# A ring of expert weights: two neighbouring pieces asked for in one 1 MB transfer instead of two of 512 KB

## The chip, the cores and the metric

The kernel runs on one core of a Trainium2 chip, as one launch. The metric is the device time of that launch in microseconds (us). Three runs of the kernel before took 1549.37, 1553.48 and 1554.05 us; their median is 1553.48 us.

## The reference, cut to what matters

The program is one layer of an encoder: modulated norm, an input projection, a retention branch and a differential attention branch, an output projection, and then a mixture of 16 experts over 640 tokens (512 of a prompt, 8 x 16 of samples). The change touches only the expert part:

```python
# hf: 640 tokens x 1024; w1, w3: 16 x 1024 x 512; w2: 16 x 512 x 1024; every token goes to 2 of the 16 experts
for e in range(N_EXPERTS):
    ff = (jax.nn.silu(hf @ w1[e]) * (hf @ w3[e])) @ w2[e]
    y = y + combine[:, e:e + 1].astype(hf.dtype) * ff
```

All of it is float32. The weights of one expert are 3 x 2 MB, so 16 experts read 100 MB of HBM, each byte once.

## The kernel before, in words

**Tiling.** An expert gets a block of up to 128 token rows, fetched by an indirect DMA from GpSimd (POOL) into `xe` and turned on TensorE (PE) into `xT`. The weights come in pieces of 128 partitions x 2 x 512 float32, 512 KB, 12 per expert: four of W3, four of the next expert's W1, four of W2. Pieces are numbered in the order of use; 0 to 3 (W1 of expert 0) have buffers of their own, 4 to 191 go through a ring of 12 slots (`RING`, line 1261; `slot`, line 1350). For an expert e from 0 to 14 W3 is pieces 12e+4 to 12e+7, W1 of e+1 is 12e+8 to 12e+11, and W2 is 12e+12 to 12e+15 (the last experts differ a little, line 1267).

**The life of a piece n.** Products of float32 are made of three matmuls on float32r parts (`mm3`, line 91), so each piece is split first:

1. SyncE (SP) waits until TensorE has used piece n-12, which had the same slot, and issues the DMA into `raw` (lines 1401 to 1403).
2. ScalarE (ACT) waits for the landing and writes the high part, `hi` (line 1454).
3. VectorE (DVE) writes the low part, `lo`, over the raw data (line 1536).
4. TensorE runs six matmuls of 512 columns (lines 93 to 95 by way of `up`, line 1639, or `down`, line 1647) and counts `used`.

Each slot has a semaphore `loaded` of its own (line 1353).

**Order on each engine.** All is written out by hand. ACT and DVE walk through steps m = 0, 1, ... and split piece m+4 in step m (`LEAD`), with their other work at fixed places between (lines 1479 to 1505 and 1575 to 1590). What matters here is the product of the two hidden activations, `multiply` (line 1553, the row L1556 of a profile): it stands on DVE right behind the low part of piece 12e+11. TensorE needs it after two of the four W1 pieces of the next expert, when it turns the product (`turn_a`, line 1631; rows L1636):

```python
for p in range(4):
    if p == 2:
        turn_a(e)                                     # waits for multiply(e)
    up(first_piece("W1", e + 1) + p, p, self.U, e + 1)
```

SP's queue also sends each expert's finished 512 KB of rows to HBM (`send_y`, line 1413), before the pieces 28, 40, 52, ... It waits before piece 8 for the token rows of expert 0 (line 1400). One more user of the DMA engines is the indirect fetch of `xe` (line 1427).

Of the kernel before, what the change touches and what calls it, by code (L numbers as in the profile page):

```python
# [24 lines left out]
F32 = mybir.dt.float32  # L25
# [7 lines left out]
P = 128  # L33
# [19 lines left out]
W = 512  # L53
# [7 lines left out]
class Map:  # L61


    def __init__(self, nc, start, end):
        self.nc, self.at, self.end = nc, start, end
# [1195 lines left out]
RING, LEAD, EARLY, PIECES = 12, 4, 12, 12 * N_EXP  # L1261
# [3 lines left out]
def first_piece(kind, e):  # L1265

    return {"W1": 12 * e - 4 if e else 0, "W3": 12 * e + (4 if e < N_EXP - 1 else 0), "W2": 12 * e + (12 if e < N_EXP - 2 else 16 if e < N_EXP - 1 else 8)}[kind]


class Experts:  # L1270


    def __init__(self, nc, io, K, ctx, banks):
        self.io, self.K = io, K
        sem = lambda name: K.semaphore("m_" + name)
        many = lambda name, n: [sem(f"{name}{i}") for i in range(n)]
        base, hT, wt = K.phase_base, K.hT_at, K.wts_at
        piece = lambda name, at, dt=F32: nc.alloc_sbuf_tensor_at("m_" + name, [P, 2, W], dt, offset=at)
        row = lambda name, at: nc.alloc_sbuf_tensor_at("m_" + name, [P, D_MODEL], F32, offset=at)
        at = [base + 49152 + 4096 * p for p in range(3)] + [base + 88064]  # L1280
        self.raw0 = [piece(f"raw_first{p}", at[p]) for p in range(4)]
        self.lo0 = [piece(f"lo_first{p}", at[p], F32R) for p in range(4)]
        self.hi0 = [piece(f"hi_first{p}", base + 4096 * p, F32R) for p in range(4)]
        at = [hT + 4096 * i for i in range(8)] + [wt + 4096 * i for i in range(4)]
        self.raw = [piece(f"raw{i}", at[i]) for i in range(RING)]
        self.lo = [piece(f"lo{i}", at[i], F32R) for i in range(RING)]
        self.gx = [[row(f"gx{a}_{t}", at[a * NT + t]) for t in range(NT)] for a in range(2)]
        hi_at = [wt + 16384 + 4096 * i for i in range(4)] + [base + 16384] + [base + 71680 + 4096 * i for i in range(4)] \
            + [base + 20480 + 4096 * i for i in range(3)]
        self.hi = [piece(f"hi{i}", hi_at[i], F32R) for i in range(RING)]  # L1290
        sb = Map(nc, hT + 32768, hT + 40960)
        self.xe = [sb(f"m_xe{i}", [P, D_MODEL], F32) for i in range(2)]
        sb = Map(nc, wt + 32768, wt + 49152)
        self.xT = [[sb(f"m_xT{i}_{n}", [P, KT, P], F32R) for n in ("hi", "lo")] for i in range(2)]
        sb = Map(nc, wt + 32768, wt + 36864)
        last_aT = tuple(sb(f"m_aT_last_{n}", [P, 4, P], F32R) for n in ("hi", "lo"))
        sb = Map(nc, base + 32768, base + 40960)
        self.su = sb("m_su", [P, W], F32)
        self.aT_hi = sb("m_aT_hi", [P, 4, P], F32R)
        self.aT_lo = sb("m_aT_lo", [P, 4, P], F32R)  # L1300
        self.aT = [(self.aT_hi, self.aT_lo)] * (N_EXP - 1)
        self.aT.append(last_aT)
        sb = Map(nc, base + 40960, base + 49152)
        self.yst = [sb(f"m_yst{i}", [P, D_MODEL], F32) for i in range(2)]
        sb = Map(nc, base + 61440, base + 71680)
        self.gt2 = sb("m_gt2", [P, 2, D_MODEL], F32)
        self.cf = sb("m_cf", [P, 5, 2, NT], F32)
        self.wv = sb("m_wv", [P, 2, NT], F32)
        self.ci = sb("m_ci", [P, 2, NT], I32)
        self.si = sb("m_si", [P, N_EXP], I32)  # L1310
        self.prod = sb("m_prod", [P, 2, NT, N_EXP], F32)
        sb = Map(nc, K.after_small, K.sbuf_end)
        self.iota = sb("m_iota", [P, P], F32)
        self.posm = sb("m_posm", [P, NT, N_EXP], F32)
        self.tok_in = sb("m_tok_in", [P, NT, 2], F32)
        self.tok = nc.alloc_sbuf_tensor_at("m_tok", [P, NT, 2], BF16, offset=sb.at)
        assert sb.at + 32 <= K.sbuf_end
        self.oh = [nc.alloc_sbuf_tensor_at(f"m_oh{e}", [P, NT, P], BF16, offset=hi_at[6 + e // 3] + 1280 * (e % 3)) for e in range(N_EXP)]
        self.U, self.V, self.Y, self.T, self.AT, self.X = banks[0], banks[1], banks[2:4], banks[4:6], banks[6], banks[7]
        self.loaded0, self.hi0_done, self.lo0_done = many("first_loaded", 4), sem("first_hi_done"), sem("first_lo_done")  # L1320
        self.loaded, self.hi_done, self.lo_done = many("loaded", RING), sem("hi_done"), sem("lo_done")
        self.used, self.rounds_done, self.posm_done = sem("pieces_used"), sem("rounds_done"), sem("places_done")
        self.oh_done, self.slots_done, self.slots_taken = map(sem, ("chosen", "slots_done", "slots_taken"))
        self.xe_zero, self.go, self.xe_in, self.consts, self.tok_done = sem("xe_zero"), sem("pool_goes_on"), many("xe_in", 2), sem("consts_in"), sem("tok_done")
        self.link = sem("dve_link")
        self.t_done, self.t_hi, self.t_lo, self.su_done, self.a_done, self.at_done, self.at_hi, self.at_lo = map(
            sem, ("x_turned", "x_hi", "x_lo", "su_done", "a_done", "a_turned", "a_hi", "a_lo"))
        self.y_taken, self.y_out, self.ci_done, self.gath = sem("y_taken"), many("y_out", 2), sem("rows_found"), many("gathered", NT)
        self.weighed, self.summed, self.gated, self.added_up = map(sem, ("weighed", "summed", "gated", "added_up"))
        self.gt2_in, self.out, self.stored, self.h2_out = sem("gt2_in"), sem("rows_out"), sem("round_stored"), sem("h2_out")  # L1330
# [5 lines left out]
    def source(self, n):  # L1336
        if n < 4:
            w, e, p = "w1", 0, n
        else:
            e, i = (n - 4) // 12, (n - 4) % 12  # L1340
            p = i % 4
            w = ("w3", "w1", "w2")[i // 4]
            if n >= first_piece("W3", N_EXP - 1):
                e, w = ((N_EXP - 1, "w3"), (N_EXP - 2, "w2"), (N_EXP - 1, "w2"))[(n - first_piece("W3", N_EXP - 1)) // 4]
            e += w == "w1"
        if w == "w2":
            return self.io[w][0, e, p % 2 * 256:p % 2 * 256 + 256, p // 2 * W:(p // 2 + 1) * W].rearrange("(k r) n -> r k n", k=2)
        return self.io[w][0, e, p * 256:(p + 1) * 256].rearrange("(r k) n -> r k n", k=2)

    def slot(self, n):  # L1350
        return (n - 4) % RING

    def piece_loaded(self, r, n):
        s, k = self.slot(n), (n - 4) // RING
        return self.loaded[s], r * (16 * len(range(s + 4, PIECES, RING))) + 16 * k + 16

    def piece_used(self, r, n):
# [33 lines left out]
    def run_sp(self, sp):  # L1391
        io = self.io
        R = self.rounds(sp)
        with sp.Fori(0, R) as r:
            for n in range(4, PIECES):
                e = (n - 28) // 12
                if n >= 28 and (n - 28) % 12 == 0:
                    self.send_y(sp, r, e)
                if n == 8:
                    sp.wait_ge(*self.rows_in(r, 0))  # L1400
                if n - RING >= 4:
                    sp.wait_ge(*self.piece_used(r, n - RING))
                sp.dma_start(self.raw[self.slot(n)][:], self.source(n)).then_inc(self.loaded[self.slot(n)], 16)
            for e in range(N_EXP - 2, N_EXP):
                self.send_y(sp, r, e)
            for t in range(NT):
                sp.wait_ge(*self.added(r, t))
                out = io["o_y_p"][0, t * P:(t + 1) * P] if t < NP_T else io["o_y_s"].rearrange("b l d -> (b l) d")
                sp.dma_start(out, self.K.x1[:, t]).then_inc(self.out, 16)
            sp.wait_ge(self.out, r * (NT * 16) + NT * 16)  # L1410
            sp.sem_inc(self.stored, 1)
# [1492 lines left out]
```

## Time and profile before

| what | value |
|---|---|
| median of 3 runs | 1553.48 us |
| the profiled execution, its own time | 1547.23 us |
| its span, first to last instruction | 1545.4 us |
| mean granted TensorE clock | 0.990 of full speed |
| TensorE busy | 96% of the span |
| VectorE, ScalarE, GpSimd busy | 53%, 42%, 18% |
| HBM traffic | 197 GB/s over the span |
| ring transfers `m_raw<-w` in the trace | 188 of 512 KB, issued between 1208.8 and 1494.8 us |

The expert part runs from about 1208 us to the end. Shares over the whole span say little about it, since VectorE and the DMA engines are far busier there than before; it has to be read in windows of one expert. Matmuls are pipelined, so a busy time on TensorE overlaps from one to the next; the distance between two starts is the pace.

### The profile page before, as it was taken

How to read it: one execution, taken by the hardware profiler on the slowest of the kernel's cores; microseconds unless marked ns; L12 is line 12 of the kernel's file. 1: busy time of each engine (PE TensorE's matmuls, PEld its weight loads, DVE VectorE, ACT ScalarE, POOL GpSimd, SP SyncE). 2: the span in 40 equal slices, each digit the busy share in tenths (PEclk: the TensorE clock that was granted, in tenths of full speed). 3: DMA queues.
4: the chain of work that ended last, by engine and by line, in shares of the span. 5: the costliest groups of instructions: out<-in, count | busy, mean ns of one | idle time of the engine just before them, and what ended most of it. 6: DMA issues, size and time to landing. Idle time of an engine off the chain costs nothing.

```text
span 1545.4 us, 21620 instructions
## 1 busy us (share of the span) xinstructions
PE 1480.2 (96%) x7914; PEld 1124.5 (73%) x7914; DVE 812.2 (53%) x1424; ACT 649.5 (42%) x1073; POOL 284.7 (18%) x174
## 2 busy tenths in 40 slices
PE   8999999999999999999999899999999999999991
PEld 6775777577757775778777676677778878888880
DVE  4332441243125312221776867755365799999995
ACT  5313311331133113312445454544232478888881
POOL 2342224222322332233000000000222100000002
PEclk9999999999999999999999999999999999999996
DMA  9554465446544654432441254154841799999986
GB/s 350 185 141 160 161 196 138 158 161 206 138 149 161 206 145 141 151 108 70 169 136 55 69 188 141 42 157 151 287 122 42 267 329 407 404 398 396 398 327 231
DMA packets 149789, 302.92 MB, mean 196 GB/s; under 512 B 15867, under 2 KB 43691, under 8 KB 149557
## 3 DMA queue, kind: packets, MB, share of 16 engines
q1 hardware_dynamic: 145942, 291.06, 55.5%
q0 software_dynamic: 3744, 10.49, 1.9%
q8 instruction: 65, 1.06, 0.3%
q14 instruction: 38, 0.31, 0.1%
HBM read 257.84 MB, written 46.81 MB: 197 GB/s over the span
## 4 chain that ended last, share of the span: by engine, by line
PE 39%; DVE 5%; DMA 4%; issue 2%; ACT 1%; POOL 0%; DVEq 0%; ACTq 0%; POOLq 0%; SPq 0%
PE pj L93 10%; PE pj L95 10%; PE pj L94 10%; DMA m_raw<-w 2%; PE d_B L2564 1%; PE d_B L2583 1%; PE d_B L2591 1%; DVE d_tmp L2282 1%; DMA ring_raw<-w_in 1%; PE d_B L2625 1%; PE d_B L2573 1%; DMA d_kc<-cache_diff_k 1%; PE d_B L2731 1%; PE d_B L1636 1%; PE d_B L2602 1%
## 5 line engine op out<-in xcount | busy, mean ns | idle before, releaser
L93 PE MATMUL pj<-ring_hi,hT_hi 128*128 128x512 f32 x880 | 367.7, 418 | 5.3 <-ACT d_q_rows L2040 2.4
L95 PE MATMUL pj<-ring_hi,hT_lo 128*128 128x512 f32 x880 | 344.9, 392 | 0.0
L94 PE MATMUL pj<-ring_lo,hT_hi 128*128 128x512 f32 x880 | 344.0, 391 | 0.0
L511 POOL TENSOR_TENSOR ring_lo<-ring_raw,ring_hi 128x1024 fp32r<-128x1024 f32 x79 | 190.9, 2420 | 497.9 <-ACT ring_hi L585 497.8
L585 ACT ACTIVATE ring_hi<-ring_raw 128x1024 fp32r<-128x1024 f32 x79 | 83.3, 1057 | 365.3 <-DMA ring_raw<-w_in 353.2
L1536 DVE TENSOR_TENSOR m_lo<-m_raw,m_hi 128x1024 fp32r<-128x1024 f32 x188 | 222.1, 1221 | 20.9 <-ACT m_hi L1454 19.5
L93 PEld LDWEIGHTS pj<-ring_hi,hT_hi 128*128 128x128 f32 x880 | 165.7, 188 | 48.6 <-issue 15.0
L1454 ACT ACTIVATE m_hi<-m_raw 128x1024 fp32r<-128x1024 f32 x188 | 192.6, 1058 | 19.1 <-DMA m_raw<-w 16.1
L95 PEld LDWEIGHTS pj<-ring_hi,hT_lo 128*128 128x128 f32 x880 | 165.3, 188 | 36.5
L94 PEld LDWEIGHTS pj<-ring_lo,hT_hi 128*128 128x128 f32 x880 | 166.0, 189 | 28.3 <-issue 1.0
L782 DVE SCALAR_TENSOR_TENSOR r_S<-r_S,g,r_sm 128x512 f32<-128x512 f32 x64 | 45.0, 744 | 137.0 <-PE r_sm L1031 137.0
L93 PE MATMUL pj<-m_hi,m_xT_hi 128*128 128x512 f32 x248 | 98.0, 395 | 0.0
L95 PE MATMUL pj<-m_hi,m_xT_lo 128*128 128x512 f32 x248 | 96.9, 391 | 0.0
L94 PE MATMUL pj<-m_lo,m_xT_hi 128*128 128x512 f32 x248 | 96.5, 389 | 0.0
L2032 ACT ACTIVATE ring_hi<-ring_raw 128x1024 fp32r<-128x1024 f32 x37 | 39.2, 1058 | 66.7 <-DMA ring_raw<-w_in 25.3
L93 PE MATMUL pj<-ring_hi,r_oT_hi 128*128 128x512 f32 x160 | 64.3, 402 | 0.0
L94 PE MATMUL pj<-ring_lo,r_oT_hi 128*128 128x512 f32 x160 | 62.6, 391 | 0.0
L95 PE MATMUL pj<-ring_hi,r_oT_lo 128*128 128x512 f32 x160 | 62.3, 389 | 0.0
L1427 POOL DMA_INDIRECT m_xe<-xg,m_si x16 | 16.7, 1044 | 234.9 <-PE d_B L1628 215.5
L95 PEld LDWEIGHTS pj<-m_hi,m_xT_lo 128*128 128x128 f32 x248 | 46.5, 188 | 9.9
L94 PEld LDWEIGHTS pj<-m_lo,m_xT_hi 128*128 128x128 f32 x248 | 46.6, 188 | 9.3
L93 PEld LDWEIGHTS pj<-m_hi,m_xT_hi 128*128 128x128 f32 x248 | 46.6, 188 | 9.0
(363 smaller groups left out, 2353.3 us busy)
## 6 DMA issues: line engine op xcount, KB each, us to landing
m_raw<-w SPq DMA_DIRECT2D x188, 512.0 KB, 10.1
ring_raw<-w_in SPq DMA_DIRECT2D x72, 512.0 KB, 3.8
r_S<-state_ret SPq DMA_DIRECT2D x64, 256.0 KB, 4.6
r_ada_raw<-w_ada SPq DMA_DIRECT2D x16, 1024.0 KB, 6.8
o_state_s<-r_S SPq DMA_DIRECT2D x64, 256.0 KB, 4.4
a_raw<-w_ada SPq DMA_DIRECT2D x8, 1024.0 KB, 12.3
ring_raw<-w_in SPq DMA_DIRECT2D x32, 256.0 KB, 3.3
ring_raw<-w_br_ret SPq DMA_DIRECT2D x16, 512.0 KB, 4.2
```

What stands on the lines that cost most here:

```text
L93: pe.matmul(out, s_hi, m_hi, start=start, stop=False)
L94: pe.matmul(out, s_hi, m_lo, start=False, stop=False)
L95: return pe.matmul(out, s_lo, m_hi, start=False, stop=stop)
L511: pool.tensor_tensor(lo[:, p], raw[:, p], hi[:, p].bitcast(F32), ALU.subtract).then_inc(lo_done, 1)
L585: act.activation(hi[:, p], raw[:, p], ACT.Copy).then_inc(hi_done, 1)
L782: dve.scalar_tensor_tensor(S[:, u % 8], S[:, u % 8], K.g16[:, h:h + 1], job_bank("U", h, u)[:], ALU.mult, ALU.add) \
L1427: pool.indirect_dma_start(out=self.xe[e % 2][:], out_offset=None, in_=self.io["xg"][0:NT * P, :], in_offset=bass.IndirectOffsetOnAxis(ap=s ...
L1454: act.activation(self.hi[self.slot(n)][:], self.raw[self.slot(n)][:], ACT.Copy).then_inc(self.hi_done, 1)
L1536: dve.tensor_tensor(self.lo[s][:], self.raw[s][:], self.hi[s][:].bitcast(F32), ALU.subtract).then_inc(self.lo_done, 1)
L1636: last = pe.transpose(self.AT[:, a * P:(a + 1) * P], self.su[:, a * P:(a + 1) * P], K.ident[:])
L2032: act.activation(hi[:, p], raw[:, p], ACT.Copy).then_inc(hi_done, 1)
L2282: links(dve.tensor_tensor(tmp[:, m].rearrange("p (g c) -> p g c", c=DDH), x, bc(tabs[:, a, t, m].unsqueeze(1), [P, 8, DDH]), ALU.mult))
```

## The change

The twelve raw buffers of the ring become six pairs at the same addresses; the pairs are pieces (4, 5), (6, 7), ... SP's loop goes in steps of two. For a pair it waits until TensorE has used the second piece's predecessor, n-11, and issues one DMA of 128 partitions x 4 runs of 512 float32, 1 MB, which counts on the semaphore of the even slot. Both pieces of a pair wait for that one semaphore. The pieces on ACT, DVE and TensorE, and their order there, stay as they are.

In W1 and W3 a partition's share of a piece is two neighbouring rows, one run of 4 KB in HBM; of a pair it is two such runs, 512 KB apart. In W2 a partition's share of a piece is two half rows of 2 KB, and of a pair four of them, each 512 KB from the next.

```diff
-        self.raw = [piece(f"raw{i}", at[i]) for i in range(RING)]
         self.lo = [piece(f"lo{i}", at[i], F32R) for i in range(RING)]
+        self.raw_pair = [nc.alloc_sbuf_tensor_at(f"m_raw_pair{i}", [P, 2, 2, W], F32, offset=at[2 * i]) for i in range(RING // 2)]
+        self.raw = [self.raw_pair[i // 2][:, i % 2] for i in range(RING)]
...
-        if w == "w2":
-            return self.io[w][0, e, p % 2 * 256:p % 2 * 256 + 256, p // 2 * W:(p // 2 + 1) * W].rearrange("(k r) n -> r k n", k=2)
+        if n >= 4:
+            if w == "w2":
+                return self.io[w][0, e, :, p // 2 * W:(p // 2 + 1) * W].rearrange("(q k r) n -> r q k n", q=2, k=2)
+            return self.io[w][0, e, p * 256:(p + 2) * 256].rearrange("(q r k) n -> r q k n", q=2, k=2)
         return self.io[w][0, e, p * 256:(p + 1) * 256].rearrange("(r k) n -> r k n", k=2)
...
     def piece_loaded(self, r, n):
-        s, k = self.slot(n), (n - 4) // RING
+        s, k = self.slot(n) // 2 * 2, (n - 4) // RING
         return self.loaded[s], r * (16 * len(range(s + 4, PIECES, RING))) + 16 * k + 16
...
-            for n in range(4, PIECES):
+            for n in range(4, PIECES, 2):
                 e = (n - 28) // 12
                 if n >= 28 and (n - 28) % 12 == 0:
                     self.send_y(sp, r, e)
                 if n == 8:
                     sp.wait_ge(*self.rows_in(r, 0))
                 if n - RING >= 4:
-                    sp.wait_ge(*self.piece_used(r, n - RING))
-                sp.dma_start(self.raw[self.slot(n)][:], self.source(n)).then_inc(self.loaded[self.slot(n)], 16)
+                    sp.wait_ge(*self.piece_used(r, n + 1 - RING))
+                sp.dma_start(self.raw_pair[self.slot(n) // 2][:], self.source(n)).then_inc(self.loaded[self.slot(n)], 16)
```

## Rows read from the trace of the kernel before

**Rows 1.** The page: busy time per engine, and the span in 40 slices.

```profile
PE 1480.2 (96%) x7914; PEld 1124.5 (73%) x7914; DVE 812.2 (53%) x1424; ACT 649.5 (42%) x1073; POOL 284.7 (18%) x174
DMA  9554465446544654432441254154841799999986
```

**Rows 2.** Windows of one expert each: window, length, busy time (instructions), TensorE clock, DMA share, GB/s.

```profile
1230.00:1248.40 18.40, 18.40 (x88) 15.37 (x87) 16.63 (x18) 15.26 (x20) 0.99 (x1) 1.00 0.97 345
1248.40:1269.10 20.70, 17.94 (x85) 14.72 (x84) 19.60 (x34) 14.66 (x19) 0.99 (x1) 1.00 0.93 330
...
1286.92:1304.72 17.80, 17.80 (x86) 14.87 (x85) 16.59 (x17) 15.08 (x19) 0.99 (x1) 1.00 1.04 405
...
1358.12:1376.25 18.13, 18.01 (x86) 14.78 (x85) 16.48 (x17) 15.57 (x19) 0.99 (x1) 1.00 1.03 398
...
1412.03:1430.47 18.44, 18.01 (x86) 14.79 (x85) 16.33 (x17) 15.43 (x19) 0.99 (x1) 1.00 1.02 396
```

**Rows 3.** TensorE's timeline, two matmuls that follow each other: start, duration.

```profile
1356.16 0.39 PE L94 MATMUL pj<-m_lo,m_aT_hi 128*128 128x512 f32 x1
1356.39 0.39 PE L95 MATMUL pj<-m_hi,m_aT_lo 128*128 128x512 f32 x1
```

**Rows 4.** Waits from 1286.92 to 1448.44 us: who waited for whom, total, times, longest.

```profile
ACT m_hi L1454 <- DMA m_raw<-w: 12.6, 29, 1.1
DVE m_lo L1536 <- ACT m_hi L1454: 12.4, 30, 0.9
PEld d_B L1636 <- DVE m_su L1556: 2.3, 5, 0.9
```

**Rows 5.** The chain of waits from 1350 to 1367 us, around piece 95.

```profile
1351.06 11.69 DMA m_raw<-w
1362.74 0.02 issue
1362.76 1.07 ACT m_hi L1454
...
1365.00 0.69 DVE m_su L1556
...
1365.74 0.66 PE d_B L1636 x4
```

**Rows 6.** The same wait three experts on: the chain from 1404 to 1422 us.

```profile
1404.97 12.00 DMA m_raw<-w
```

**Rows 7.** Issues and landings of all DMAs from 1290 to 1440 us.

```profile
m_raw<-w SPq DMA_DIRECT2D x101, 512.0 KB, 10.4
yg<-m_yst SPq DMA_DIRECT2D x8, 512.0 KB, 10.8
```

**Rows 8.** SP's own waits over the span: who waited for whom, total, times, longest.

```profile
SPq L1403 <- PE pj L95: 177.9, 168, 8.0
```

**Rows 9.** ACT's timeline: two high parts without a wait.

```profile
1266.27 2.00 ACT L1454 ACTIVATE m_hi<-m_raw 128x1024 fp32r<-128x1024 f32 x2
```

**Rows 10.** DVE's timeline: the low parts of pieces 94, 95 and 96, 97.

```profile
1362.70 2.38 DVE L1536 TENSOR_TENSOR m_lo<-m_raw,m_hi 128x1024 fp32r<-128x1024 f32 x2 [0.57 <-ACT m_hi L1454]
...
1365.60 2.36 DVE L1536 TENSOR_TENSOR m_lo<-m_raw,m_hi 128x1024 fp32r<-128x1024 f32 x2
```

**Rows 11.** DVE's and TensorE's timelines: the product and its turn, experts 3 and 12.

```profile
1292.42 0.68 DVE L1556 TENSOR_TENSOR m_su<-m_su,pj 128x512 f32<-128x512 f32 x1
...
1294.26 0.60 PE L1636 MATMUL d_B<-ident,m_su 128*128 128x128 f32 x4
...
1454.98 0.68 DVE L1556 TENSOR_TENSOR m_su<-m_su,pj 128x512 f32<-128x512 f32 x1
...
1455.78 0.60 PE L1636 MATMUL d_B<-ident,m_su 128*128 128x128 f32 x4
```

**Rows 12.** SP's timeline: the issues of pieces 34 to 39.

```profile
1260.68 8.18 SPq L1403 DMA_DIRECT2D m_raw<-w  x6
```

**Rows 13.** DMA from 1262 to 1275 us, 40 slices of 0.325 us.

```profile
GB/s 366 416 429 403 315 277 252 315 340 328 164 82 44 107 233 246 265 221 233 164 170 277 340 397 397 378 366 303 265 63 82 139 158 258 366 353 353 384 422 410
```

## The prediction

> **What bounds the kernel now.** The page comes first, to find the stage. TensorE is busy for 96% of the span, VectorE for 53%, and the last slices of the DMA row, where the experts are, stand at 9, which nothing before them does for long [rows 1]. So the expert part is unlike the rest, and only its own windows count.
>
> The windows come next. From 1287 us an expert takes 17.80 us, and TensorE is busy through all of it, at a granted clock of 1.00; but the DMA share is 1.04 at 405 GB/s and VectorE works 16.59 us [rows 2]. Three resources are within 7% of one another. TensorE's pace is read from two starts, 0.23 us apart (0.227 over many), so a piece of six matmuls takes 1.36 us [rows 3]; twelve make 16.3, and turning rows and products takes the rest of 17.80. Some windows are longer, 18.13 and 18.44 us, with TensorE busy for 18.01 in both and the data at 396 to 398 GB/s [rows 2].
>
> The waits say who is late. Between 1287 and 1448 us ACT waited 29 times for a landing, 12.6 us in all; DVE waited 30 times for ACT, 12.4 us; TensorE's side lost 2.3 us, in five waits for the product L1556 [rows 4]. The chain shows how: piece 95 is issued at 1351.06, lands 11.69 us later, ACT splits it, DVE splits it, and only then comes the product (1365.00) that TensorE turns at 1365.74 [rows 5]. Piece 131 does the same with 12.00 us [rows 6].
>
> Is a landing slow by latency or by a queue? A ring transfer takes 10.4 us in the median from 1290 to 1440 us [rows 7], and one is issued about every 1.48 us (17.80 / 12), so about seven are on their way at any time, while the engines already move 400 GB/s. That is a full queue. Its rate is the landing pace; the time of an issue hardly matters while something is queued.
>
> The loss by it is small. Expert 3 turned its product at 1294.26. Nine experts of 17.80 would put expert 12's turn at 1454.46; it was at 1455.78 [rows 11]. TensorE lost 1.3 us to weights in that stretch, and no change to the ring can gain more there.
>
> **What the change does, part by part.**
>
> *Fewer issues.* SP issues 94 transfers instead of 188. SP is not late: 168 times it waited at this line for TensorE, 177.9 us [rows 8]. Nothing; the cover is SP's own waiting.
>
> *A full queue moves the same bytes.* Descriptors of 4 KB and 2 KB stay what they are. From a queue seven pieces deep, the bytes of piece n arrive when they did. I take 0 for the rate itself, and bound it: a gain of 1.3 us at most, all that TensorE loses now; a loss by the rival below.
> The Trainium skill ("DMA: Bandwidth & Descriptors", section Bandwidth) advises batching to 1 MiB or more for 75% of peak and has 341 GB/s for a transfer of 1 MB by itself. The trace disagrees for queued transfers: pieces of 512 KB already move at 405 GB/s [rows 2]. By the page's rule the time would fall; by the row it does not.
>
> *The even piece tells of itself one piece later.* Piece 94 now counts as landed when 95 has. The two then come to ACT together. ACT starts two high parts 0.95 us apart (2.00 for two less 1.05 for one [rows 9]), DVE two low parts 1.14 to 1.16 apart (2.36 or 2.38 for two less 1.22 for one [rows 10]). With L the landing of 95, 1362.74: before, hi 95 at L + 0.02, its low part at L + 1.12 (hi takes 1.07 [rows 5]), the product at L + 2.26. After, hi 94 starts at L + 0.02, so low 94 at L + 1.12, low 95 at L + 2.26, the product at L + 3.38. The product comes 1.12 us later relative to the same bytes.
> What hides it? In expert 3 the product started at 1292.42 and could have been turned at 1293.15 (0.68 and 0.05 more); it was turned at 1294.26, so there was 1.11 us of room, just enough [rows 11]. In expert 12 it started at 1454.98, 1455.71 against 1455.78: room 0.07 [rows 11]. So the 1.12 us comes through in full but for 0.07: +1.05 us. It is paid once, not per expert: once TensorE is 1.05 us later, every next product has that room again, since the landings do not move. The rows of the last expert are fetched two experts ahead, so near the end the engines have less to move and TensorE paces alone; the delay stays.
>
> *The issue of the even piece comes 1.36 us later.* It waits for the use of n-11, not n-12. Behind this wait on SP stand the next pieces and the finished rows (`send_y`); rows are needed two experts later, so nothing. In the full queue nothing either: 10 us are ahead of it. It costs where the queue is empty. That is once in the stage, at 1262 to 1268 us: TensorE stood still behind DVE's long list (19.60 us of work in a window of 20.70 [rows 2]), SP could issue piece 34 only at 1260.68 [rows 12], and a little later the DMA moves 44 to 107 GB/s [rows 13]. Pair (34, 35) leaves at about 1262.05 and the hole grows by up to 1.36 us; every later byte is that much later. Between 0 (something else was in the way, as the low slices at the end of these rows suggest) and 1.36 I take 1.0, near the upper end, because the slices of 44 to 107 GB/s show an idle engine. It adds in full, since the landings are what the product waits for from expert 4 on.
>
> *The start.* Pieces 4 to 15 wait for no use. TensorE is busy all through the window 1230 to 1248 us, at 345 GB/s: no landing is late there, so I take nothing. If one were, it would be by a piece, 1.36 us, once.
>
> **Sum:** 0 + 1.05 + 1.0 = +2.05 us; 0 to +2.4 with the bounds of the two terms, 1.36 more with the start's, -1.3 with a gain in the rate. Made against the profiled execution that is 1547.2 to 1549.3 us, a span of 1545.4 to 1547.5. That execution lies 6.3 us below the median of the three runs (1553.48), which spread over 4.7 us; I carry the difference over: 1555.5 us. A measurement here tells from no change what exceeds about 0.3%, 4.7 us, so this is "no difference".
>
> **Rivals.**
>
> *A: hidden or better.* The pair's queue runs a little better (fewer completions to tell of), the landings come ahead of need, and the 1.12 us falls into room. Then TensorE paces throughout and 1.3 us come back: 1552.2 us. For it: only tenths of a microsecond an expert are missing now. Against it: 405 GB/s leaves nothing that the trace shows as a gap between transfers. This is also where the page's rule would lead, as far as this kernel lets it: TensorE's 17.80 us is the floor whatever the DMA does. Chance 0.25.
>
> *B: slower, by the order of the reads.* A pair's descriptors alternate between places 512 KB apart, four of them for W2. If HBM serves that order worse, a full queue passes it on at once. Its place is the W2 third of each expert, 2.1 MB. At 405 GB/s that takes 5.2 us; at the 330 GB/s of the window 1248 to 1269 [rows 2], the lowest that pieces were moved at over a whole expert, 6.4. Nine experts from 1287 to 1448 us would lose 10.6 us, with the forecast's 2.05 some 1566 us. For it: rows show slices of 63 to 158 GB/s at 1271.8 to 1273 us, with four W2 pieces on their way, so W2 can be slow [rows 13]. Against it: each engine already took W2 in two alternating places, and the windows are at 405 all the same. It passes the 4.7 us from 0.3 us an expert on, W2 at 383 GB/s. Chance 0.18.
>
> *The change does nothing*, because the hardware cuts a 1 MB transfer as it cuts two of 512 KB: the cutting may be the same, but the wait for both halves is in the program, so the forecast's terms stand. No case of its own.
>
> **How the numbers follow.** Forecast 0.57, A 0.25, B 0.18. The time is the forecast's, 1555.5. A median of few runs can be off by some 2 us either way (half the spread). The range goes down to 1550.5, A's 1552.2 less most of that, and up to 1561, the forecast plus about half of B. Forecast and A lie inside 4.7 us of 1553.48 unless the measurement is off: 0.76 within, 0.06 faster, by scatter alone; B and the forecast's upper tail make 0.18 slower.
>
> **What would show it.** Right: 94 issues of 1024 KB, issue to landing some 11 to 12 us; the DMA share still 1.02 to 1.04 at about 400 GB/s; ACT's waits for landings fewer but longer, followed by two high parts without a gap; waits of TensorE for L1556 from expert 4 on, about 2 us more of them than the 2.3 of before; the turn of expert 12 at 1457 to 1458 us. Wrong: windows above 18.3 us one after another at under 390 GB/s (B); windows of 17.80 throughout (A); or a wait at another place, such as TensorE for a low part itself.

## The result, and the profile after

Twenty runs of each kernel: the changed one has a median of 1554.36 us, the one before 1551.24 us; the ratio is 1.0024 with a 95% interval of 1.0015 to 1.0033, so the change costs 3.7 us (2.3 to 5.1). The forecast was 1555.5 us and +2.05 us, "no difference": the time and the sign hold, and the whole interval of the cost lies above the sum. That the time came within 1.2 us is partly luck: the three runs that it was built on have a median of 1553.48 us, 2.2 us above that of the twenty.

The profiled execution took 1551.46 us, with a span of 1549.6 us, 4.2 us longer than before. Where do they lie? The starts of four matmuls cut the expert part: the first of piece 4, those of pieces 46 and 154, each right behind a turn of the product (experts 3 and 12), and that of piece 191. Pieces 46 and 154 after the change, from TensorE's timeline (start, duration):

```profile
1296.03 0.48 PE L93 MATMUL pj<-m_hi,m_xT_hi 128*128 128x512 f32 x1
...
1460.33 0.47 PE L93 MATMUL pj<-m_hi,m_xT_hi 128*128 128x512 f32 x1
```

And before:

```profile
1294.62 0.48 PE L93 MATMUL pj<-m_hi,m_xT_hi 128*128 128x512 f32 x1
...
1456.13 0.47 PE L93 MATMUL pj<-m_hi,m_xT_hi 128*128 128x512 f32 x1
```

Cut by these starts, in us:

| | start to piece 4 | 4 to 46 | 46 to 154 (nine experts) | 154 to 191 | after it |
|---|---|---|---|---|---|
| before | 1229.6 | 65.0 | 161.5 | 53.9 | 35.4 |
| after | 1231.0 | 65.0 | 164.3 | 53.9 | 35.4 |

1.4 us come from ahead of the experts, where no line differs; that part came out between 1229.2 and 1238.5 in the profiles of this study, more than their whole spans differ (1545.4 to 1553.0). The rest, 2.8 us, lies wholly in the nine experts. Nine at 17.80 are 160.2: the kernel before loses 1.3 there, the changed one 4.1. So this stretch is the sharp measure below, beside the ratio of the timed runs.

The same windows after, one expert each (columns as in [rows 2]):

```profile
1288.32:1306.13 17.81, 17.81 (x86) 14.88 (x85) 16.60 (x17) 14.98 (x19) 0.99 (x1) 1.00 1.03 401
...
1341.88:1360.26 18.38, 18.01 (x86) 14.79 (x85) 16.26 (x17) 15.37 (x19) 0.99 (x1) 1.00 1.02 391
...
1378.57:1397.34 18.77, 18.02 (x86) 14.79 (x85) 16.50 (x17) 15.21 (x18) 0.99 (x1) 1.00 0.97 377
```

The first of these windows still has 17.81 us, and the two behind it 17.80 and 17.95. From 1341.88 on the loss comes with every expert, 0.3 to 1.0 us each, where before it came with some. The waits from 1288.32 to 1451.94 us:

```profile
ACT m_hi L1457 <- DMA m_raw_pair<-w: 19.4, 21, 1.8
DVE m_lo L1539 <- ACT m_hi L1457: 16.4, 28, 1.5
PEld d_B L1639 <- DVE m_su L1559: 4.8, 7, 1.2
PE d_B L1639 <- DVE m_su L1559: 1.8, 5, 0.7
```

Before, from 1286.92 to 1448.44 us, beside those of [rows 4]:

```profile
PE d_B L1636 <- DVE m_su L1556: 0.4, 1, 0.4
```

So there are fewer but longer waits for landings, and more for the product. The two halves of a pair come together, as the timelines of ACT and DVE show at pieces 94 and 95:

```profile
1363.93 2.01 ACT L1457 ACTIVATE m_hi<-m_raw_pair 128x1024 fp32r<-128x1024 f32 x2 [1.81 <-DMA m_raw_pair<-w]
```

```profile
1365.03 2.36 DVE L1539 TENSOR_TENSOR m_lo<-m_raw_pair,m_hi 128x1024 fp32r<-128x1024 f32 x2 [1.45 <-ACT m_hi L1457]
1367.31 0.68 DVE L1559 TENSOR_TENSOR m_su<-m_su,pj 128x512 f32<-128x512 f32 x1
```

From landing (1363.83) to product it is 3.48 us, where before it was 2.26 [rows 5]: 1.2 us more, against 1.12 forecast. What was not forecast is the chain of waits. From 1350 to 1440 us, before and then after, shares of the stretch by line:

```profile
by line: DMA m_raw<-w 26.3%; PE pj L95 20.4%; PE pj L93 20.3%; PE pj L94 20.2%; PE d_B L1636 3.3%; issue 2.6%; ACT m_hi L1454 2.4%; PE d_B L1628 1.6%; PE pj L1628 1.6%; DVE m_su L1556 1.5%; DVE m_lo L1536 0.1%; DVEq L1535 0.1%
```

```profile
by line: DMA m_raw_pair<-w 59.3%; DVE m_lo L1539 7.1%; issue 6.4%; ACT m_hi L1457 5.9%; PE pj L95 5.3%; PE pj L93 5.1%; PE pj L94 5.1%; PE d_B L1639 3.6%; DVE m_su L1559 2.7%; DVEq L1558 0.2%; DVEq L1538 0.2%; ACTq L1454 0.2%
...
1353.19 10.64 DMA m_raw_pair<-w
...
1371.51 11.11 DMA m_raw_pair<-w
...
1390.27 10.54 DMA m_raw_pair<-w
...
1408.48 10.60 DMA m_raw_pair<-w
...
1426.74 10.46 DMA m_raw_pair<-w
```

Five experts in a row, each landing of the pair (12e+10, 12e+11) leads to the product, the product to the turn, the turn and two pieces to the next issue of that same pair. The ring has closed on itself: 18.32 us from 1353.19 to 1371.51, of which 10.64 are the landing and 7.68 the way back. Before, the way back was 6.44 us (1351.06 to the next issue at 1369.19, less 11.69). To keep a period of 17.80, a landing may take 11.4 us before and 10.1 us after. The five above took 10.5 to 11.1.

The landing is no constant of the queue, though. By SP's issues and the landings' semaphore, piece 12e+11 of experts 3 to 7 took 9.9, 10.7, 10.9, 11.0 and 11.7 us before, and its pair 9.4, 10.0, 10.3, 10.7 and 10.6 after. At a period of 17.80 it grows from expert to expert, until it has used up what the ring can bear; the changed kernel gets there about two experts sooner.

### The profile page after: what moved, and what is told of

Same layout as the page of the kernel before. It is cut to its first block, busy times and chain, and to the rows that moved or that the text cites. A ratio compares the mean times of both kernels' runs of the same rounds, so it can differ in the third digit from the quotient of the medians.

```text
span 1549.6 us, 21438 instructions
## 1 busy us (share of the span) xinstructions
PE 1481.2 (96%) x7914; PEld 1124.2 (73%) x7914; DVE 811.4 (52%) x1424; ACT 646.1 (42%) x1073; POOL 284.1 (18%) x174
## 4 chain that ended last, share of the span: by engine, by line
PE 34%; DMA 8%; DVE 6%; issue 2%; ACT 2%; SPq 1%; POOL 0%; DVEq 0%; ACTq 0%; POOLq 0%
PE pj L93 8%; PE pj L95 8%; PE pj L94 8%; DMA m_raw_pair<-w 5%; PE d_B L2567 1%; PE d_B L2586 1%; DMA d_kc<-cache_diff_k 1%; PE d_B L2594 1%; DVE d_tmp L2285 1%; PE d_B L2628 1%; DMA ring_raw<-w_in 1%; DVE m_lo L1539 1%; PE d_B L2576 1%; PE d_B L1639 1%; PE d_B L2734 1%
## 5 line engine op out<-in xcount | busy, mean ns | idle before, releaser
L1539 DVE TENSOR_TENSOR m_lo<-m_raw_pair,m_hi 128x1024 fp32r<-128x1024 f32 x188 | 221.3, 1220 | 25.1 <-ACT m_hi L1457 24.2
L1457 ACT ACTIVATE m_hi<-m_raw_pair 128x1024 fp32r<-128x1024 f32 x188 | 188.2, 1054 | 29.9 <-DMA m_raw_pair<-w 26.4
```

Source lines behind the costliest of these rows:

```text
L1457: act.activation(self.hi[self.slot(n)][:], self.raw[self.slot(n)][:], ACT.Copy).then_inc(self.hi_done, 1)
L1539: dve.tensor_tensor(self.lo[s][:], self.raw[s][:], self.hi[s][:].bitcast(F32), ALU.subtract).then_inc(self.lo_done, 1)
```

## The experiments

Each kernel below was timed in eleven or twelve runs (both_two_transfers in five) beside the kernel before. "Nine experts" is the stretch from piece 46 to 154 in its one profile. Where a kernel was profiled twice, the two agree within 0.2 us.

| kernel | nine experts, us | ratio (95%) |
|---|---|---|
| before | 161.5 | 1 |
| after | 164.3 | 1.0024 (1.0015 to 1.0033) |
| after_again | 164.3 | 1.0014 (1.0003 to 1.0025) |
| late_issue | 161.9 | 1.0012 (1.0001 to 1.0023) |
| late_ready | 161.8 | 1.0016 (1.0005 to 1.0027) |
| both_two_transfers | 164.7 | 1.0036 (1.0022 to 1.0049) |
| both_two_again | 164.7 | 1.0018 (1.0008 to 1.0028) |
| pairs_but_one | 161.9 | 1.0018 (1.0007 to 1.0029) |
| one_pair_only | 161.2 | 1.0005 (0.9993 to 1.0018) |
| light_w2_singles | 160.2 | 0.9995 (0.9984 to 1.0005) |
| light_w2_pairs | 160.2 | 0.9995 (0.9984 to 1.0006) |
| product_early_singles | 160.4 | 0.9990 (0.9979 to 1.0002) |
| product_early_singles_again | 160.2 | 0.9986 (0.9976 to 0.9997) |
| product_early_pairs | 161.6 | 1.0010 (0.9998 to 1.0023) |

### Which part of the change costs?

The change does three things: a later issue, a joint arrival, a larger transfer. Each of the first two alone, both without the third, and the whole:

```diff
# late_issue, against the kernel before
-                if n - RING >= 4:
-                    sp.wait_ge(*self.piece_used(r, n - RING))
+                if n - RING >= 4 and n % 2 == 0:
+                    sp.wait_ge(*self.piece_used(r, n + 1 - RING))
# late_ready, against the kernel before; both_two_transfers has both edits
                 act.wait_ge(*self.piece_loaded(r, n))
+                if n % 2 == 0:
+                    act.wait_ge(*self.piece_loaded(r, n + 1))
```

> The kernel before, with 512 KB transfers and a semaphore for each piece, but both pieces of a pair issued only after the use of n-11; nothing else of the change. The even piece still tells of itself alone. Theory R (the loss comes from the even piece's joint arrival): +0 to +0.5 us against the kernel before, expert windows near 17.9 to 18.0 as before. Theory I (the late issue costs, since the ring's own loop issue, landing, split, product, use is what sets the pace): +2 us or more of the 3.1. Theory D (the 1 MB transfer moves its bytes more slowly): +0.

> The kernel before, with its 512 KB transfers issued at their old times; only ACT waits, for an even piece, for the landing of its partner too. Theory R: +1.1 to +3 us, the product later by 1.1 us against the landing of piece 12e+11, as in the kernel after. Theory I: +0 to +0.5. Theory D: +0 to +0.5.

> Late issue and joint arrival together, but still two transfers of 512 KB: the change without its 1 MB transfer. If R and I are all there is, this equals the kernel after (+3.1 us, 1.002). If D holds, it is faster than the kernel after by the part that the reads' order costs: +1 to +2 us, with the windows from expert 6 on at 396 to 405 GB/s instead of 388 to 391.

> The changed kernel itself on this chip, as the measure for the three others: +3 us (1.0015 to 1.0033) by every theory.

> Late issue and joint arrival with two transfers of 512 KB, as in both_two_transfers, for a second measurement. If the 1 MB transfer by itself gives something back: slower than the changed kernel, 1.003 or more. If the first number was scatter: 1.002, like the changed kernel's 1.0024 and 1.0014.

The larger transfer does nothing by itself: with two transfers of 512 KB the stretch is 164.7, with one of 1 MB 164.3, and the timed ratios overlap (1.0018 and 1.0036 against 1.0014 and 1.0024). Theory D, and with it rival B of the prediction, falls. The waits of both_two_again for the product are much like those of the kernel after:

```profile
PEld d_B L1638 <- DVE m_su L1558: 5.5, 8, 1.1
PE d_B L1638 <- DVE m_su L1558: 2.5, 4, 0.7
```

Neither R nor I is right alone. In the stretch, the late issue adds 0.4 us, the joint arrival 0.3, and the two together 3.2. In late_ready the chain from 1350 to 1440 us goes by a landing only once, and landings have less than half of their share before:

```profile
by line: PE pj L95 25.5%; PE pj L93 25.4%; PE pj L94 25.2%; DMA m_raw<-w 12.2%; PE d_B L1638 3.2%; PE d_B L1630 2.1%; PE pj L1630 2.1%; DVE m_lo L1538 1.4%; issue 1.4%; ACT m_hi L1456 1.2%; DVE m_su L1558 0.7%; DVEq L1557 0.0%; DVEq L1537 0
...
1408.97 10.96 DMA m_raw<-w
```

Yet the way back from landing to next issue is as long there: 7.7 us from expert 6 on, as in the changed kernel. What differs is the landing of piece 12e+11: from expert 6 to 11 it took 10.1 to 10.3 us in late_ready (once 10.96), and 10.5 to 11.1 us in the changed kernel. So with the joint arrival alone the landing shortened to nearly what the ring could bear; with the late issue as well it did not.

The timed ratios of the two, 1.9 and 2.5 us with intervals of 1.7 us to each side, would also fit a plain sum: 4.4 us, where the four timings of both together gave 2.2 to 5.6. They hold all that happens in a launch, and the stretch has one profile each. That the parts reinforce each other is what the profiles say; the times do not decide it.

### Is it the load?

The traffic of an expert is cut by 7%, while the engines keep their instructions and sizes: two of its four W2 pieces load only one of their two rows, the high part is made of that row twice, and the low part is the high part less itself, so part of W2 is left out of the computation. (A first form of this, with one eighth of each expert's finished rows sent to HBM, gave no time and no profile.)

```diff
# light_w2_singles, against the kernel before (light_w2_pairs: three of a pair's four rows)
+                k = 1 if 16 <= n < 180 and (n - 4) % 12 in (9, 11) else 2
+                sp.dma_start(self.raw[self.slot(n)][:, 0:k], self.source(n)[:, 0:k]).then_inc(self.loaded[self.slot(n)], 16)
...
+                if self.light(n):                           # in ACT's high_part; the same pieces
+                    source = bc(source[:, 0:1], [P, 2, W])
...
+                source = self.hi[s][:].bitcast(F32) if self.light(n) else self.raw[s][:]      # in VectorE's low_part
```

> The kernel before, with 7% less traffic: of two of the four W2 pieces of an expert (12e+13 and 12e+15, from piece 16 on) only the first of two rows is loaded, and the high part is made of it twice (so the output is not the layer's); ACT, VectorE and TensorE keep their instructions and sizes. Theory F (a full DMA queue is behind the waits): the queue drains, issue to landing falls from 10.4 us to 6 or less, windows of 17.80 us, 1.3 us gained. Theory L (waits come from latency, not load): landings stay over 9 us and waits for the product L1556 stay.

> The changed kernel with the same cut: of the pairs (12e+12, 12e+13) and (12e+14, 12e+15) three of four rows are loaded. Theory F: within 0.7 us of the run with single pieces, all of the change's loss gone. Theory L: 3 us slower than that run.

In the stretch the whole loss of both kernels goes, and with it the difference between them. TensorE is busy for all of 80 us, at 372 GB/s with single pieces, and just so at 368 GB/s with pairs:

```profile
1360.00:1440.00 80.00, 80.00 (x377) 66.75 (x376) 74.10 (x72) 67.44 (x82) 3.96 (x4) 1.00 0.99 372
```

From 1290 to 1440 us, a 512 KB piece now lands in 6.3 us in the median (10.4 before), a pair of 1 MB in 7.6 (10.3 after). This is the sharpest of the results: with room in the queue, late issue and joint arrival cost nothing in the stretch, and the timed ratios of the two are the same.

### Is it the one pair in front of the product?

Pieces 12e+10 and 12e+11 are the ones that the product stands behind. pairs_but_one takes only them out of the change; one_pair_only gives only them both waits, with two transfers.

```diff
# pairs_but_one, against the kernel after (the source and the semaphore of these two pieces are as before)
...
+                if (n - 4) % 12 == 6:
+                    for one in (n, n + 1):
+                        if one - RING >= 4:
+                            sp.wait_ge(*self.piece_used(r, one - RING))
+                        sp.dma_start(self.raw[self.slot(one)], self.source(one)).then_inc(self.loaded[self.slot(one)], 16)
+                    continue
# one_pair_only, against the kernel before
+                if n - RING >= 4 and not (n > 16 and (n - 4) % 12 == 7):
+                    sp.wait_ge(*self.piece_used(r, n - RING + ((n - 4) % 12 == 6)))
...
+                if (n - 4) % 12 == 6:
+                    act.wait_ge(*self.piece_loaded(r, n + 1))
```

> The changed kernel, but pieces 12e+10 and 12e+11 are two transfers of 512 KB with semaphores of their own, each issued after the use of its own predecessor; the ten others of an expert stay in pairs. If the loss sits at this pair alone, in front of the product: 0 to +0.7 us against the kernel before, and a wait for the product about as before (2.3 us to 1448 us). If late issue at any pair starves the queue: +2 us or more stays.

> The kernel before; only pieces 12e+10 and 12e+11 get what the change does, late issue and joint arrival, and still as two transfers of 512 KB; the ten others are as before. The converse of pairs_but_one. If the loss sits at this pair, where the late issue falls on the pause that the turn of the product makes in SP's issues and the joint arrival on the product itself: nine experts (piece 46 to 154) take 163.5 to 164.7 us instead of 161.5. If it needs all six pairs: 161.9 or less.

pairs_but_one takes 161.9 us in the stretch, near the kernel before, but its timed ratio is 1.0018, 2.8 us (1.1 to 4.5) where up to 0.7 was expected, and as much as the changed kernel's. So its two measures contradict each other, and the one profile may not be the common case. one_pair_only takes 161.2 us, no slower than the kernel before, and its ratio agrees: of its two expectations "it needs all six pairs" came true. The pair alone is not enough, then; that is shown by both measures. That it is needed is what the stretch says and the times do not. Which wait of the five others counts, no run separates.

The trace of one_pair_only shows how the pair does no harm: the way back is 8.1 to 8.5 us from expert 6 on, longer than in the changed kernel, but its pieces 12e+11 landed in 9.3 to 9.7 us, and once in 10.6, in the one expert that took 18.7.

### Is it the product's place?

```diff
# product_early_singles against the kernel before; product_early_pairs has the same edit
-                    if i == (4 if e < N_EXP - 1 else 0):
+                    if i == (3 if e < N_EXP - 1 else 0):
                         multiply(e)
```

> The kernel before, with VectorE's product one step earlier, ahead of the low part of piece 12e+11 instead of behind it. If the landing of that piece reaches TensorE only by way of the product, the 1.3 us of waits for it go: windows of 17.80 us throughout, 0.999 of the time before. If the weights themselves are late, windows of 18 us and more stay and TensorE waits for L1536 instead.

> The changed kernel with the same move of the product. If the joint arrival costs by way of the product, the loss goes nearly whole: within 0.5 us of the run with single pieces and the product early, 0.999 to 1.000 of the kernel before. If the late issue starves the queue by itself, some 2 us against that run stay, with DMA rates of 388 to 391 GB/s in the windows from expert 6 on.

> The kernel before with the product one step earlier, a second time, to see whether it beats the kernel before: nine experts in 160.2 to 160.4 us as in its first run, piece 4 to 46 in 64.0 or 65.6 us (with or without the drop of the clock), ratio 0.998 to 0.9995.

With single pieces the 1.3 us go (160.4 and 160.2), and 1.0 us more in expert 1, where TensorE waits for the product behind a long list on VectorE: 1.62 us there instead of 2.76, in the timelines of product_early_singles_again

```profile
1266.33 0.66 PE L1636 MATMUL d_B<-ident,m_su 128*128 128x128 f32 x4 [1.62 <-DVE m_su L1556]
```

and of the kernel before:

```profile
1258.61 0.66 PE L1636 MATMUL d_B<-ident,m_su 128*128 128x128 f32 x4 [2.76 <-DVE m_su L1556]
```

Both ratios are below 1, the second with its interval. This version is faster than the kernel before, by some 2 us. In the two profiles the landings of pieces 12e+11 grow to 12.6 and 12.3 us by expert 11, and TensorE waits for the product no more than 0.4 us in all: it no longer stands behind them.

With pairs, the stretch falls from 164.3 to 161.6 us, but the loss has not gone nearly whole, as was expected. Against single pieces with the product early the stretch is still 1.2 us longer, nearly all of it in one expert of 18.9 us; pieces 154 to 191 take 54.8 us instead of 53.9; and the median of the timed runs is 3.6 us longer (1551.89 against 1548.29), where 0.5 was expected. TensorE still waits for the product three times in the stretch, 1.7 us. So in the timed runs pairs cost about as much with the product early as with it late, and what they cost there no experiment here isolates.

## Why the prediction was right or wrong, point by point

- **A full queue, and TensorE just ahead of it.** Right, and shown by light_w2_singles: 7% less traffic, and no wait for a landing or for the product is left. The issue to landing forecast for the pairs, 11 to 12 us, was 10.3 in the median.
- **The rate of the 1 MB transfer, 0.** Right within 0.4 us. The Trainium skill ("DMA: Bandwidth & Descriptors", section Rules for kernel authors) advises 1 MiB or more per DMA for bandwidth; no run here shows a gain from it in a queue that is already full. The same list advises to issue a DMA early and to wait for it late, to overlap it with compute; the change does the opposite twice, and both_two_again, 164.7 us against 161.5 in the stretch, agrees with that rule.
- **The joint arrival, +1.12 us on the way to the product.** The size was right: 1.2. The step that failed is "It is paid once, not per expert", with its reason, "since the landings do not move". The landings did move. They hang on the issues, the issues on TensorE's use, and this on the product: once the way back has grown from 6.44 to 7.68 us, the landing that the ring can bear is 10.1 us, and each expert pays what the landing takes beyond it, 0.3 to 1.0 us at the five landings above. Taken alone (late_ready) the joint arrival cost only 0.3 us in the stretch, less than forecast, since there the landing was 10.2 us in the median from expert 6 on.
- **The late issue, "in the full queue nothing either".** That failed as well, by the same loop. Alone it adds 0.4 us to the stretch; beside the joint arrival it is the difference between 161.8 and 164.7. So the forecast also failed in adding up two terms that the profiles show to depend on each other. Near the turn SP now issues nothing for 4.2 us (1386.10 to 1390.27; before, 2.3 at the same turn, 1387.05 to 1389.39), and some microseconds later the DMA runs dry in part. In the changed kernel:

```profile
1395.60:1397.40 1.80, 1.80 (x9) 1.50 (x8) 1.74 (x2) 1.59 (x4) 0.00 (x0) 1.00 0.64 232
```

  It is no single case. Of windows of 1.80 us, one every 0.6 us from piece 82 to piece 154, 6 of 181 are below 300 GB/s in the changed kernel, 5 to 8 in after_again and in the two kernels with both waits and two transfers, 3 in late_issue, and none in the kernel before or in late_ready, whose lowest are 323 and 314 GB/s. So such holes come with the late issue, and they are more with both. A queue whose transfers land in 10 us in the median can still be empty on some of its 16 engines: the DMA share is 0.64 in the row above. I read the median landing as the depth of all of them. That the holes are how the late issue spoils the rate is argued from this, not shown by a run of its own.
- **The hole at 1262 to 1268 us, +1.0 us.** Wrong: 0. Piece 4 to piece 46 takes 65.0 us before and after. The pair (34, 35) did land late, but by expert 3 the landing of piece 47 stood 5.4 us ahead of the first matmul of piece 46, 4.9 before. The total came near because this term made up for part of the one above: that is luck.
- **The turn of expert 12 at 1457 to 1458 us.** It was at 1459.92; less the 1.4 us from ahead of the experts, 1458.5.
- **Rival A**, hidden or better: wrong, the first loss comes with expert 4, 17.94 us from turn to turn. **Rival B**, the order of the reads: wrong.

What stays open: how late issue and joint arrival share the loss in a timed launch; why pairs_but_one loses little in its profile and 2.8 us in its timed runs; and what the pairs still cost once the product is early.

## What to carry to other kernels

When a ring feeds an engine through a queue that is just full, add up the loop from issue to issue of one slot (landing, the work in between, the use), and compare it with the period at which the ring must turn. Once no room is left, every turn pays what the landing takes beyond it. But do not take the landing as a constant: here it ran from some 9 to 12.6 us in full queues, and time added to the loop cost little alone (0.3 us) and much together with a late issue (3.2 us). A larger transfer had no value here, where smaller ones already queued, and it brought a later issue and a later arrival. Work in order on an engine that depends on early data should stand ahead of work that depends on the latest landing: one step earlier for the product gained some 2 us with single pieces, of which 1.0 lay at expert 1 and the rest in the ring.

## What the runs showed of the hardware

TensorE's clock can drop after a pause of 2.77 us. In late_ready it stood still that long, until 1261.02, at a granted clock of 1.00, and from 1262.0 to 1265.4 us the granted clock was half, 1.2 instead of 2.4 GHz. The windows' last three numbers are clock, DMA share and GB/s:

```profile
1260.00:1262.00 2.00, 0.98 (x7) 0.90 (x8) 2.00 (x3) 0.29 (x1) 0.00 (x0) 1.00 1.03 420
1262.00:1264.00 2.00, 2.00 (x6) 1.60 (x5) 2.00 (x4) 2.00 (x3) 0.00 (x0) 0.50 1.02 408
1264.00:1266.00 2.00, 2.00 (x8) 1.55 (x7) 2.00 (x2) 0.20 (x1) 0.00 (x0) 0.65 0.91 336
```

Pieces 4 to 46 then take 66.6 us instead of 65.0. It happened in six of the eleven profiles that have this pause at its full length (2.76 to 2.77 us), in kernels with and without pairs, and in one of the two profiles of the same kernel with both waits and two transfers; in the three whose pause was cut to 1.6 us it did not. It is not what keeps the stretch of late_issue and late_ready short, since both_two_again had the drop as well and took 164.7 us.
